# Two narrow stretches of two weight units in place of four of one, in the expert layers of a two-block transformer kernel

## What is computed

```python
def grouped_moe(x, w_router, router_bias, w1, w3, w2):
    ...
    g_sel = jnp.argmax(group_score, axis=-1).astype(jnp.int32)     # one of 8 groups of 4 experts
    in_group = jnp.take_along_axis(biased, g_sel[:, None, None], axis=1)[:, 0]
    local = lax.top_k(in_group, TOP_K)[1]                          # 2 experts of it
    ...
    def expert_block(args):
        xb, e = args
        hid = jax.nn.silu(xb @ w1[e]) * (xb @ w3[e])
        return hid @ w2[e]
```

## Time and profile before

| what | us |
|---|---|
| median of three runs | 2207.65 |
| the profiled execution | 2207.64 |
| its span, first to last instruction | 2205.8 |
| PE busy | 2076.7 (94%) |
| DVE busy | 1159.4 (53%) |
| ACT busy | 767.2 (35%) |

### The profile page before, as it was taken

How to read it: one execution, slowest core, us unless ns; L and a number is a source line. 1 busy time by engine, 2 the same in 40 slices (tenths; PEclk the granted TensorE clock), 3 DMA queues, 4 the chain that set the end, 5 groups by cost and what they waited for, 6 DMA issues and landing times.

```text
span 2205.8 us, 28498 instructions
## 1 busy us (share of the span) xinstructions
PE 2076.7 (94%) x11724; PEld 1636.6 (74%) x11724; DVE 1159.4 (53%) x1729; ACT 767.2 (35%) x1183; POOL 63.5 (3%) x98
## 2 busy tenths in 40 slices
PE   5999999999999999999999799999899999899996
PEld 3677787888897699889998655556599987555563
DVE  4333333377784265565656633357666466423475
ACT  3111122355433144444443222234335432212251
POOL 0000000010010000000001100000000002000000
PEclk8999999999999999999999999999999999899998
DMA  9655523122341345434423179989453332689894
GB/s 367 257 218 218 205 77 124 38 77 77 119 169 77 147 166 180 165 139 155 153 98 132 52 290 376 379 336 384 184 180 134 115 134 71 241 338 379 336 387 187
DMA packets 55328, 433.60 MB, mean 197 GB/s; under 512 B 7328, under 2 KB 8608, under 8 KB 17696
## 3 DMA queue, kind: packets, MB, share of 16 engines
q1 hardware_dynamic: 51344, 423.35, 50.2%
q10 hardware_dynamic: 3856, 8.42, 1.1%
HBM read 430.71 MB, written 1.05 MB: 196 GB/s over the span
## 4 chain that ended last, share of the span: by engine, by line
PE 56%; issue 35%; DVE 5%; DMA 2%; ACT 1%; DVEq 1%; POOL 0%; POOLq 0%; SPq 0%; ACTq 0%
PE bank L2894 33%; PE bank L3639 4%; PE bank L2887 3%; PE bank L3637 3%; PE bank L3690 2%; PE bank L2830 1%; PE bank L3701 1%; PE bank L3050 1%; DMA ring<-in_l_moe_in 1%; PE bank L3688 1%; PE bank L3563 1%; DMA ring<-in_early 1%; PE bank L3654 1%; DVE ring_lo L2748 1%; DVE X L2738 1%
## 5 line engine op out<-in xcount | busy, mean ns | idle before, releaser
L2894 PE MATMUL bank<-HT_LO,ring_lo 128*128 128x256 f32 (+1 forms) x992 | 287.6, 290 | 0.0
L2894 PE MATMUL bank<-X_HI,ring_lo 128*128 128x256 f32 x1472 | 270.7, 284 | 2.1 <-issue 2.1
L2894 PE MATMUL bank<-HT_HI,W_HI 128*128 128x512 f32 (+1 forms) x704 | 238.7, 339 | 7.0 <-DVE ring_lo L1915 4.0
L2894 PE MATMUL bank<-HT_HI,ring_lo 128*128 128x512 f32 (+1 forms) x704 | 240.3, 341 | 0.0
L2894 PE MATMUL bank<-HT_LO,W_HI 128*128 128x512 f32 (+1 forms) x704 | 238.3, 339 | 0.0
L2894 PEld LDWEIGHTS bank<-X_HI,ring_lo 128*128 128x128 f32 x1472 | 230.6, 190 | 3.9 <-issue 3.8
L1199 ACT ACTIVATE W_HI<-ring 128x2048 fp32r<-128x2048 f32 x66 | 126.3, 1914 | 285.2 <-PE bank L2894 225.7
L2894 PEld LDWEIGHTS bank<-HT_LO,ring_lo 128*128 128x128 f32 x992 | 187.9, 189 | 3.2 <-issue 0.5
L1915 DVE TENSOR_TENSOR ring_lo<-ring,W_HI 128x2048 fp32r<-128x2048 f32 x66 | 151.0, 2288 | 66.0 <-ACT W_HI L1199 65.9
L2282 DVE TENSOR_TENSOR ring_lo<-ring,ring_lo 128x2048 fp32r<-128x2048 f32 (+2 forms) x64 | 143.2, 2247 | 42.3 <-ACT ring_lo L1452 41.2
L2894 PEld LDWEIGHTS bank<-HT_HI,W_HI 128*128 128x128 f32 x704 | 133.5, 190 | 28.6 <-issue 9.8
(11 more groups left out here) (541 smaller groups left out, 3708.7 us busy)
## 6 DMA issues: line engine op xcount, KB each, us to landing
ring<-in_early SPq DMA_DIRECT2D x54, 2048.0 KB, 8.4
ring<-in_l_moe_in SPq DMA_DIRECT2D x36, 2048.0 KB, 14.1
ring<-in_l_dense SPq DMA_DIRECT2D x62, 1024.0 KB, 4.9
ring<-in_l_moe_out SPq DMA_DIRECT2D x14, 2048.0 KB, 13.9
ring<-in_early SPq DMA_DIRECT2D x23, 1024.0 KB, 4.7
slot<-in_l_moe_in SPq DMA_DIRECT2D x10, 2048.0 KB, 10.1
slot_xg<-in_l_moe_in SPq DMA_DIRECT2D x10, 2048.0 KB, 12.0
HT<-in_l_moe_in SPq DMA_DIRECT2D x8, 2048.0 KB, 9.1
```

The costliest lines, as they stand in the source:

```text
L2894: last = mm(out, a, b, start=start and n == 0, stop=stop and n == 2)
```

## The change

`FOUR_BEHIND` names two places in place of four, and at each place two units of rank 7 are loaded in a row. `four_parts` makes the products of both units in one stretch, with one drain before and one behind.

```diff
-FOUR_BEHIND = ((1, 1), (1, 3), (2, 0), (2, 1))
+FOUR_BEHIND = ((1, 3), (2, 1))
...
             if (rank, e) in FOUR_BEHIND:
-                parts[len(hidden)] = len(ins)
-                ins.append(add("in", 7, 0, len(ins)))
+                parts[len(hidden)] = (len(ins), len(ins) + 1)
+                ins += [add("in", 7, 0, len(ins) + a) for a in range(2)]
...
-                def four_part(i):
+                def four_parts(some):
 
                     h = HIDDEN[FOUR]
                     pe.drain()
-                    ps = take(J_UP[FOUR]) if i == 0 else PS[J_UP[FOUR][0]]
-                    w = weights(h.ins[i]).rearrange("p (e k n) -> p e k n", e=PER_GROUP, n=BANK)
-                    for k in range(2 * i, 2 * i + 2):
-                        for a in range(PER_GROUP):
-                            q = a * h.size
-                            last = mm(ps[q:q + h.size, :], TOKENS[:, k, SLOTS_AT[7]:SLOTS_AT[7] + h.size], w[:, a, k % 2, :],
-                                      start=k == 0, stop=k == KD - 1, tile_position=(0, q))
-                    if i < PER_GROUP - 1:
-                        freed(h.ins[i], last)
-                    else:
-                        last.then_inc(*full(J_UP[FOUR]))
+                    ps = take(J_UP[FOUR]) if 0 in some else PS[J_UP[FOUR][0]]
+                    for i in some:
+                        w = weights(h.ins[i]).rearrange("p (e k n) -> p e k n", e=PER_GROUP, n=BANK)
+                        for k in range(2 * i, 2 * i + 2):
+                            for a in range(PER_GROUP):
+                                q = a * h.size
+                                last = mm(ps[q:q + h.size, :], TOKENS[:, k, SLOTS_AT[7]:SLOTS_AT[7] + h.size], w[:, a, k % 2, :],
+                                          start=k == 0, stop=k == KD - 1, tile_position=(0, q))
+                        if i < PER_GROUP - 1:
+                            freed(h.ins[i], last)
+                        else:
+                            last.then_inc(*full(J_UP[FOUR]))
                     pe.drain()
...
                     if n in FOUR_PARTS:
-                        four_part(FOUR_PARTS[n])
+                        four_parts(FOUR_PARTS[n])
```

## The result

The changed kernel takes **2220.81 us** (median of 6 runs, 2220.22 to 2227.12), the kernel before 2207.89 in the same comparison. The ratio is 1.0064, with a 95% interval from 1.0052 to 1.0075: slower by some 13 us, where 2218.7 was forecast. The profiled execution took 2220.82 us, its span 2219.0.

The account below looks back on a forecast made before the run. PE, 94% busy, was taken as the bound, with the loads neck and neck. Step 24's delays of 4.0 and 3.65 us plus 3.4 of clock made +11.05 on 2207.64: 2218.7 us, range 2211 to 2224.

Parts of the forecast that it names:

- Where the burst starts: Load in(2,1), freed by step 18's down products, starts the burst: taken as unmoved, ends -0.8 to +1.8 us per layer.
- What the unit costs: 7.2 joins the burst before in(2,3), 16 MB in place of 14; in(2,3) lands 5.1 us later at 410 GB/s.
- the dip of the DMA share: Sign: DMA share dips between about 1508 and 1516 us, ahead of the burst, then is full to about 1555.
- The rows' loads: Rival: ACT's two 512 KB loads delay in(2,3) by up to 2.6 us per layer; 0.10 together with a longer clock fall.
- Step 24: Its raw products wait for in(2,3) and start 4.0 us later in the first layer, 3.65 in the second.
- The smaller waits for 7.3 and out 7.1: Before step 24: out 7.1 lands near 1549.4, the second stretch may wait for 7.3; smaller waits swallowed by the last.
- The clock: Behind step 24's wait: 3.4 us at half clock, 1.7 us lost per layer, 3.4 in all.
- The win on PE: Each of two merges per layer saves PE 2.53 - 1.77 = 0.76 us; 3.0 us at most over both layers.
- Step 17's own gain: Step 17 loses a stretch of 2.53 us, of which 1.6 counted as won (between 0 and 2.5) because of DVE.
- The rival that ends not slower: in(2,3) lands before PE reaches step 24, so only the merges show: 2204.6 us; chance 0.14.

Follow-up runs that it names:

- down_first: Changed kernel with the down products of the step before placed ahead of each narrow stretch, no longer behind it; 2209.36 us, ratio 1.0003 to the kernel before.
- rows_late: Changed kernel with ACT's two 512 KB loads of the second normalisation's rows issued one step later; 2217.87 us, ratio 1.0053 to the kernel before.
- second_pair: Changed kernel with only 7.2 and 7.3 merged, 7.0 and 7.1 in stretches of their own as before; 2213.07 us, ratio 1.0026 to the kernel before.
- clock_held2: Changed kernel with 5 spare products ahead of step 24's up products in each layer, keeping PE at work in the wait; 2216.50 us, ratio 1.0041.

## Why the prediction was right, point by point

- **Where the burst starts.** Taken as unchanged; in(2,1) goes out 33.38 us after step 17's first product before and 33.28 after. In the second layer both are 33.3 to 33.4. Right, and down_first shows that this start decides: sooner by 4.3 us, and the cost is gone.
- **What the unit costs.** Forecast 5.1 us for the landing of in(2,3), measured +5.88 and +5.65 from the same zero (1537.28 + 19.1 - 1478.51 = 77.87, before 1537.83 + 13.8 - 1479.64 = 71.99; in the second layer 77.22 and 71.57). This is the term that was too small, by 0.8 and 0.55. The bytes and the full rate were right; what was missing is the start. I took 7.2 as done when the burst began and did not count out(2,0); in fact 7.2 landed at 1513.23 and out(2,0) at 1515.70, and they kept the engines at work. Now the burst starts from rest, at 153 GB/s in its first three microseconds in place of 273. That puts off 0.36 MB, which at 421 GB/s is 0.9 us (in the second layer, 169 in place of 298, the same 0.9). With 5.0 us for the unit at 421 GB/s this makes 5.9 us, for 5.88 and 5.65 measured. It is a count of bytes from the traces; no run tests the start alone. The prediction foresaw the dip of the DMA share ahead of the burst, but gave it no price in the sum. The rows' loads, a rival that I gave little, have a small part at most: they now go out five us ahead of the landing, before three. The Trainium skill, DMA: Bandwidth & Descriptors, section Issuing engines are not separate DMA queues, says that loads issued by ScalarE, SyncE and GpSimd run on the same 16 DMA engines and interleave. The trace agrees: 0.22 and 0.20 MB of the rows' loads moved before in(2,3) was complete, and rows_late, without them, is 0.68 and 0.37 us sooner.
- **Step 24.** Forecast +4.0 and +3.65 us, measured +4.90 and +4.29: the term above, and 0.1 us from landing to product. The smaller waits for 7.3 and out 7.1 came where expected and are swallowed. For out 7.1 the reason is another than the one forecast: it was not only pushed back in the queue, it is issued 12 us later (57.66 us after step 17's first product, before 45.54), because it now takes the slot of out(2,0). The engines stay full all the same, so this cost nothing here; in second_pair it did.
- **The clock.** Forecast 3.4 us at half, 1.7 lost, in each layer. The second layer did just that; the first fell while PE was still waiting and cost 2.50. clock_held2 measures both together as 4.3 us. So the three shortfalls, 0.90 and 0.64 at step 24 and 0.80 of clock, all go one way: 13.39 us in the trace for a forecast of 11.05, and no error hid another. The Trainium skill, TensorE: Matmul & The Clock Gate, section HAM oscillation — how this bites in real kernels, counts the loss as half of the time at the low clock; 5.07 and 3.40 us of products at 0.50 that lost 2.50 and 1.70 agree.
- **The win on PE.** 0.76 us for a merge: the second unit starts 1.72 us behind the first, close to the 1.77 of the prediction. Where no wait swallows it, it shows as 0.63 to 0.73 us for the second pair (0.79 and 0.83 against the kernel before with the same order of products), and nearly not at all for the first, whose place in step 17 is taken by a wait of 0.79 us for DVE. Step 17's own gain was 1.9 us (its down products came 19.07 us after its first product and now come 17.16 after), where 1.6 was counted.
- **The rival that ends not slower** (the tail hidden after all) was given the right point: a burst that starts some 5 us earlier. down_first does so, by 4.3, and ends at the time of the kernel before, though not the 3.0 us under it that the merges alone were to win.

## What to carry to other kernels

Where weights go through a ring of slots in a fixed order, two loads in a row are not the same as two loads apart. Look for the load that waits for a slot: what stands ahead of it moves while PE works, what stands behind it joins the queue that PE will wait for, and so the price of such a move is its bytes at the rate of that stretch, and the slow start of a queue that has run empty (0.9 us here). If a step must carry more work, put the products that free a slot ahead of that work. A wait of some us on PE is to be priced with the slow products behind it.

## What the runs showed of the hardware beyond what was expected

What the clock takes behind a wait differs from layer to layer and from execution to execution. It fell behind PE's waits of 4.13, 3.95, 3.78 and 2.89 us ahead of step 24, and did not behind those of 0.85 to 2.03 us; five spare products in the wait kept it at 1.00. But in the change it was at 0.50 for 6.8 us in one layer and for 3.4 in the other, and second_pair had the fall in one of its two profiled executions, the one with the longer wait. So a median can stand above what a single trace accounts for: of second_pair's loss, 3.9 us by its median, its first profile shows less than one at step 24.
